# Which of four weight slots each load of layer 0's feed-forward stage takes

## What is computed

```python
mod = cond @ ada_w[l] + ada_b[l]
shift_m, scale_m, gate_m, shift_f, scale_f, gate_f = jnp.split(mod[:, None, :], N_MOD, axis=-1)
...
h = rms_norm(x, ffn_norm_g[l]) * (1.0 + scale_f) + shift_f
y = (silu(h @ w_gate) * (h @ w_up)) @ w_down     # 1024 -> 2816 -> 1024, layer 0
x = x + gate_f * y
```

## Time and profile before

| what | value |
|---|---|
| median of 3 runs | 2766.43 us |
| lowest and highest | 2760.78 and 2767.92 us |
| span of the profiled execution, first to last instruction | 2759.3 us |
| TensorE matmul busy | 2679.2 us, 97% of the span |
| VectorE busy | 1031.1 us, 37% |
| ScalarE busy | 445.7 us, 16% |
| DMA, mean over the span | 228 GB/s |
| mean granted TensorE clock | 0.989 |

### The profile page before, as it was taken

One profiled execution on the slowest core, in us unless ns is written; L12 is line 12 of the kernel. 1 busy time (PEld: TensorE's weight loads), 2 busy tenths in 40 slices (PEclk: granted clock), 3 DMA queues, 4 the chain that ended last, 5 costly groups with the idle time before them and its releaser, 6 DMA issues.

```text
span 2759.3 us, 40733 instructions
## 1 busy us (share of the span) xinstructions
PE 2679.2 (97%) x18164; PEld 1423.6 (52%) x18164; DVE 1031.1 (37%) x2114; ACT 445.7 (16%) x957; POOL 1.8 (0%) x25
## 2 busy tenths in 40 slices
PE   6989999999999999999999998999999999989998
PEld 4548747433333333343334445648887445564883
DVE  3433467311111111111102777836666332264034
ACT  1110002200000010000002534321110023423000
POOL 0000000000000000000000000000000000000000
PEclk9999999999999999999999999999999999999999
DMA  9848874499989999999992441013443432112542
GB/s 316 311 170 301 320 260 160 160 386 384 406 348 398 392 358 400 380 391 366 390 394 82 153 183 63 33 61 122 153 152 123 175 130 87 61 63 92 168 150 78
DMA packets 241693, 629.47 MB, mean 228 GB/s; under 512 B 13540, under 2 KB 95720, under 8 KB 230248
## 3 DMA queue, kind: packets, MB, share of 16 engines
q1 hardware_dynamic: 241512, 626.81, 60.6%
HBM read 625.72 MB, written 1.05 MB: 227 GB/s over the span
## 4 chain that ended last, share of the span: by engine, by line
PE 91%; DVE 3%; DMA 2%; SPq 2%; ACT 1%; issue 1%; DVEq 0%; ACTq 0%
PE banks L1797 21%; PE banks L1817 10%; PE banks L1619 9%; PE banks L1578 9%; PE banks L1698 8%; PE banks L1281 6%; PE banks L1339 5%; PE banks L1178 3%; PE banks L1545 3%; PE banks L1660 2%; PE banks L1138 2%; PE banks L911 2%; DMA sb_weights<-ada_w 1%; PE banks L1768 1%; SPq L672 1%
## 5 line engine op out<-in xcount | busy, mean ns | idle before, releaser
L1797 PE MATMUL banks<-sb_weights,sb_arena 128*32 128x512 f32 x3072 | 340.1, 593 | 0.2 <-ACT sb_arena L2309 0.2
L1619 PE MATMUL banks<-sb_hT,sb_weights 128*128 128x256 f32 x1152 | 255.2, 384 | 8.5 <-issue 6.1
L1797 PE MATMUL banks<-sb_arena 128*32 128x256 f32 (+1 forms) x3072 | 256.7, 486 | 0.0
L1619 PEld LDWEIGHTS banks<-sb_hT,sb_weights 128*128 128x128 f32 x1152 | 220.9, 192 | 42.7 <-issue 9.0
L1698 PE MATMUL banks<-sb_weights,sb_arena 128*128 128x512 f32 x528 | 229.4, 594 | 1.5 <-ACT sb_gate_bc L1947 1.5
L3218 DVE TENSOR_TENSOR sb_hT<-sb_hT,banks 128x256 f32<-128x256 f32 (+1 forms) x96 | 37.3, 388 | 488.7 <-ACT sb_hT L2319 475.0
L1797 PEld LDWEIGHTS banks<-sb_weights,sb_arena 128*32 128x32 f32 x3072 | 99.0, 110 | 226.4 <-issue 225.4
L1797 PEld LDWEIGHTS banks<-sb_arena 128*32 128x32 f32 x3072 | 99.0, 110 | 147.8 <-issue 116.2
L1817 PE MATMUL banks<-sb_weights,sb_hT 128*32 128x512 f32 x1536 | 166.3, 592 | 0.0
L1698 PEld LDWEIGHTS banks<-sb_weights,sb_arena 128*128 128x128 f32 x528 | 99.4, 190 | 125.8 <-issue 123.9
L1281 PE MATMUL banks<-sb_weights,sb_hT 128*128 128x512 f32 (+1 forms) x400 | 160.7, 559 | 1.4 <-ACT sb_mod_rows L2059 1.4
(11 more groups left out here) (348 smaller groups left out, 2839.0 us busy)
## 6 DMA issues: line engine op xcount, KB each, us to landing
sb_weights<-moe_w_gate SPq DMA_DIRECT2D x64, 1024.0 KB, 15.0
sb_weights<-moe_w_up SPq DMA_DIRECT2D x64, 1024.0 KB, 17.1
sb_weights<-moe_w_down SPq DMA_DIRECT2D x64, 1024.0 KB, 13.1
sb_weights<-w_mod SPq DMA_DIRECT2D x48, 1024.0 KB, 7.0
sb_arena<-moe_w_gate SPq DMA_DIRECT2D x48, 1024.0 KB, 11.4
sb_arena<-moe_w_up SPq DMA_DIRECT2D x48, 1024.0 KB, 13.5
sb_arena<-moe_w_down SPq DMA_DIRECT2D x48, 1024.0 KB, 16.5
sb_weights<-w_ffn_in SPq DMA_DIRECT2D x44, 1024.0 KB, 7.7
```

What stands on the lines that cost most here:

```text
L1619: mm = pe.matmul(dst, ring[j][:, k, lo:lo + P], hT[:, k, 0:T * P], start=(k == 0), stop=(k == KC - 1))
L1797: mm = pe.matmul(psum[32 * q:32 * q + 32, r % 2, 0:2 * w], ex_hT[:, k, half * CAP + g * GROUP:half * CAP + (g + 1) * GROUP], wts[:, q, :, ...
```

## The change

Loads 19 to 56 and 57 to 62 get a slot from a table. Gate/up and down loads (but for the last, down 5) take slots 3 and 0 in alternation; modulation and late loads, down 5 and load 56 take slots 1 and 2 in alternation. Nothing else is touched: the order of loads on SP, their sizes, and the order of work of every engine stay. Loads 19 to 23 keep the slots they had, and the layers 2 and 3 (g = 1) are not affected.

```diff
+        BY_KIND = {17: 3, 18: 0}
+        for n, i in enumerate((19, 20, 23, 26, 28, 31, 33, 36, 38, 41, 43, 46, 48, 50, 52, 54)):
+            BY_KIND[i] = (3, 0)[n % 2]
+        for n, i in enumerate((21, 22, 24, 25, 27, 29, 30, 32, 34, 35, 37, 39, 40, 42, 44, 45, 47, 49, 51, 53, 55, 56)):
+            BY_KIND[i] = 1 + n % 2
+        BY_KIND.update({57: 3, 58: 0, 59: 1, 60: 0, 61: 2, 62: 3})
+
         def slot_of(g, i):
 
             if g == 0:
-                return {17: 3, 18: 0, 61: 2, 62: 3}.get(i, i % SLOTS)
+                return BY_KIND.get(i, i % SLOTS)
```

## The result

The changed kernel takes 2775.64 us, the median of 4 runs (2774.98 to 2780.6), against 2763.61 us for the kernel before in the same count of runs. The medians lie 12.0 us apart. The ratio is 1.0051, interval 1.0034 to 1.0068, which is some 14 us. Timed again in a later batch, it took 2778.38 us with a ratio of 1.0064 (1.005 to 1.0077), some 18 us more. It is slower, by 12 to 18 us; I had worked out 11.1.

The account below looks back on a forecast made before the run. TensorE, busy through nearly all of the 2759.3 us span, was taken as the bound; new waits add 11.1 us (span 2770.4), plus 7.1 us from span to run median gives 2777.5 us, range 2768.0 to 2786.0.

Parts of the forecast that it names:

- the list: Layer 0, gate/up 3 to down 1: predicted later start of each block, from 1.8 us at block 3 to 11.1 us.
- The prices: Gate/up and down loads on SP: landing 11.0 us behind a late load, 13.3 us behind a modulation load, counted from the release.
- the sum: Gate/up 3 to down 1: block shifts reach 11.1 us, which stay to the end, for a span of 2770.4 us.
- rival 2: TensorE's new waits in layer 0: slow clock follows them, 5.1 us more, 16.2 us in all, 2782.6 us; chance 0.12.
- the lower bound of 11.2 us: Gate/up behind a modulation load: four DMAs of 1.05 MB at 373 GB/s can't land sooner than 11.2 us.
- Layer 1: Layer 1's mixer: load 60 waits for the pool columns but lands at 460.6, before 461.80, so no cost; cover 1.2 us.
- Rival 1: Layer 0's gate/up and down loads: the queue hides most waits, 2.5 to 8.3 us slower, say 2771.5 us; chance 0.24.
- Rival 3: Block 3: gate/up 3 goes when slot 0 is free, its wait vanishes, 8.4 us less, 2758.0 us; chance 0.04.

Follow-up runs that it names:

- the best kernel: Changed kernel with SP issuing next gate/up or down load first, then late, then modulation load, late loads taking slots long given back: 2752.98 us, 0.9976 to the kernel before.
- the kernel with matmuls ahead of block 8: Changed kernel plus two idle matmuls, about 2.4 us, into an unused bank ahead of the wait for gate/up 8: 2778.0 us, ratio 1.0064 to the kernel before.
- change from load 44 on: Kernel before with the slots by kind only from load 44 on, four slots in turn up to load 43: 2761.97 us, ratio 1.0009.

## Why the prediction was right, and where it was off

**The mechanism** is shown. "The wait on VectorE isn't removed, it moves from the gate/up load to the load ahead of it": SP's waits say just that, the late load 25 went out at 198.87 with gate/up 3 at 199.72, and changing nothing but the order in the line moves the time by 37 us.

**The places.** Waits at blocks 3, 5, 7, 8, 10 and down 1 and none at 4 and 9, block 8 the dearest: right. The down product began at 346.29 and not near 341. A wait at block 6 of 0.6 us did not appear, since block 5 was already later than the list had it. Down 0 had none for the same reason.

**The sizes** were too small, 11.1 us against 16.5 at the stage's end in the profile and 12 to 18 in the runs. In the profiled pair the shifts were, mine and measured: block 3 1.8 and 2.2, block 5 2.8 and 4.8, block 7 4.7 and 6.7, block 8 7.5 and 10.3, block 10 8.6 and 14.1, down 1 11.1 and 16.5. The errors add up from block to block, since a release moves with the chunks. Two terms make them:

- *The prices.* From the first issue of the load ahead to the landing of gate/up I took 11.0 us behind a late load and 13.3 behind a modulation load. The listed landings of the changed kernel, at blocks 5 and 8 (the up half, issued at 234.89 and 280.79):

```profile
sb_weights<-ffn_w_up SPq DMA_DIRECT2D x1, 1024.0 KB, 10.0
...
sb_weights<-ffn_w_up SPq DMA_DIRECT2D x1, 1024.0 KB, 13.3
```

  give 234.89 + 10.0 - 232.84 = 12.1 us and 280.79 + 13.3 - 279.45 = 14.6 us. Read in the same way at the other places it is 11.6, 10.9 and 11.2 us behind late loads and 13.3 and 14.1 behind modulation loads of gate/up, 12.7 and 12.9 for down. So the down price was too high and the gate/up prices too low, by 0.5 us in the mean behind a late load and 0.7 behind a modulation load, most at block 8, where it counts most. My 13.3 was one row, in which modulation load 32 had left 3.6 us ahead of gate/up 6. Whether that distance is the reason isn't shown: at block 6 of the changed kernel the two left together and took 13.3 all the same.
- *The clock.* I put it at zero in the sum and at 5.1 us in rival 2. In the profile it is 0.4 us more at blocks 3 and 4 (30.45 against 30.08) and 1.9 us at block 8 (15.77 against 13.9). Rival 2 was thus partly true: 2.3 us here, and more in the repeated run. Of the 5.4 us that the list lacks at down 1, these are 2.3; the rest is the prices. The 3.0 us of slow clock in layer 3's mixer stand in no list at all.

**The range** held the time, and the 2777.5 us lie within 2 us of it, partly by luck: I added 11.1 us to a base of 2766.43, and more runs put the kernel before at 2760 to 2763.6. That base stands 7.1 us above the profiled span, but in every run on record an execution's time is only about 1.8 us above its own span: the rest of the 7.1 was the spread of the three runs. With 1.8 us the same sum gives 2772.2. The two errors cancel in the time, not in the difference. One reading was wrong without bearing on the sum: 373 GB/s wasn't the highest rate seen, since the earlier trace rows themselves have 421 over 3 us, by which the lower bound of 11.2 us would be 10.0.

**Layer 1** costs nothing: right. Load 60 came in time, and the 16.5 us stay constant past the u columns.

**Rival 1**, the queue hides it, fell with sizes above mine. **Rival 3**, faster, fell here, but its mechanism is what makes the best kernel: there gate/up 3 goes out when its slot is free, the 6.1 us wait and the slow clock behind it are gone, and I had priced that at 8.4 us; the kernel is 7.5 us faster by the medians. Its stage is 9.5 us shorter, but 1.7 of these are chunk 4, which kept full clock behind its 2.2 us wait there.

## What to carry to other kernels

Giving a stream its own slots doesn't free it while one queue issues all loads in order: the wait sits in the queue, so look at every claim ahead of the load you care about, and ask who gives that slot back. Separate slots make another order of issue possible; the gain is in the order, and every load that the critical engine reads must go ahead of claims that wait for another engine, the small ones too. (Issuing the two kinds of load from two engines would part the lines as well; no run here tried it.) Price a queued load from a row in which both went out together, and carry the small idle times as possible slow-clock stretches. Before a time is laid to the change, see where in the trace it arises: 3 us of a profile can come from a slow stretch far behind it.

## What the runs showed that I had not expected

The granted clock doesn't follow from the length of a wait alone. After waits of 1.45 us it never fell. After 1.8 to 2.9 us it sometimes fell, with some 1.6 to 1.7 us lost (2.9 in one case), and sometimes not: a wait of 1.94 us at block 7 was followed by slow chunks (the kernel with matmuls ahead of block 8), one of 1.82 us at the same place was not (the change), and 2.75 us ahead of down 0 were not either (change from load 44 on). After 3.25 us and more ahead of a gate/up load it was low each time. Ahead of a late load it wasn't always low at once: the 16 records of late load 25 behind its 3.02 us wait still took 1.07 us, as without a wait, and the clock fell within the next us of idling. By rows, TensorE was at 0.50, its 1.2 GHz level, from 208 us, still inside the broken wait ahead of block 3 of the changed kernel, to 214 us, 3.5 us into the block (columns as in the earlier trace rows):

```profile
208.00:211.00 3.00, 0.48 (x1) 0.50 (x2) 0.00 (x0) 0.00 (x0) 0.00 (x0) 0.50 1.09 405
211.00:214.00 3.00, 3.00 (x8) 2.36 (x7) 0.00 (x0) 0.00 (x0) 0.00 (x0) 0.50 1.00 413
214.00:217.00 3.00, 3.00 (x11) 2.45 (x10) 0.00 (x0) 0.00 (x0) 0.00 (x0) 0.71 1.07 348
```

The Trainium skill, "TensorE: Matmul & The Clock Gate", section "HAM oscillation — how this bites in real kernels", tells of a kernel that waited some 3 to 5 us for each next slice of its operand and started every following tile at the low clock. The waits of 3.25 us and more ahead of gate/up loads here agree with it; it has no waits as short as the 1.94 us behind which the clock was low here too.
